# Second layer's gates computed during the second gather and kept in device memory

## The reference, cut to what matters

```python
hd = project_heads(h, w_in[l], rope)          # aq ak av bq bk bv cq ck cv ga gb gc
def merge_branches(hd, ya, yb, yc, wa, wb, wc, wo):
    m = (sigmoid(hd["ga"]) * (ya @ wa) + sigmoid(hd["gb"]) * (yb @ wb)
         + sigmoid(hd["gc"]) * (yc @ wc))
    return m @ wo
x = x + gt1 * merge_branches(...)
h2 = rms_norm(x, g_norm2[l]) * (1.0 + sc2) + sh2
x = x + gt2 * peer_ffn(h2, ...)               # u[e], v[e] of 128 experts for each token
```

## Time and profile before

| | |
|---|---|
| median of 3 runs | 3022.74 us (3022.44 to 3031.11) |
| the profiled execution's own time | 3023.13 us, its span 3021.3 us |
| busy: PE, PE weight loads, DVE, ACT, POOL | 77%, 44%, 61%, 40%, 29% of the span |
| moved by DMA | 1011.33 MB, 335 GB/s in the mean |
| granted TensorE clock, mean | 0.876 of full speed |

### The profile page before, as it was taken

The page is one execution under the profiler, slowest core; times in us unless marked ns, Lnnn a source line. Parts: engine busy times, 40 slices in busy tenths (PEclk is TensorE's granted clock), DMA queues, the critical chain, the costliest instruction groups (busy, mean ns, idle before and its releaser), DMA issues.

```text
span 3021.3 us, 33356 instructions
## 1 busy us (share of the span) xinstructions
PE 2316.5 (77%) x11428; PEld 1343.9 (44%) x11428; DVE 1832.7 (61%) x4465; ACT 1214.4 (40%) x3357; POOL 864.1 (29%) x794
## 2 busy tenths in 40 slices
PE   6999998878779997966555779978998855555555
PEld 4787897434335653521111235426898511111111
DVE  3328655785665556368887645445854777776544
ACT  4215533344653234344344533334643443433333
POOL 0000001333233333334444434320000444444442
PEclk8999998989989998977777899989999987777777
DMA  6631245989999999999999999983153999999996
GB/s 273 222 127 49 90 163 220 416 339 418 421 421 419 420 421 411 413 378 421 406 420 405 419 421 421 421 336 129 46 181 139 396 421 421 421 413 421 417 421 269
DMA packets 139705, 1011.33 MB, mean 335 GB/s; under 512 B 15632, under 2 KB 15760, under 8 KB 17168
## 3 DMA queue, kind: packets, MB, share of 16 engines
q0 software_dynamic: 112032, 810.08, 65.0%
q1 hardware_dynamic: 27216, 196.45, 16.9%
q10 hardware_dynamic: 288, 2.69, 0.2%
HBM read 1008.10 MB, written 1.05 MB: 334 GB/s over the span
## 4 chain that ended last, share of the span: by engine, by line
PE 43%; DMA 30%; DVE 14%; ACT 6%; POOL 3%; issue 3%; ACTq 0%; SPq 0%; POOLq 0%; DVEq 0%
DMA att<-experts_in,att 28%; PE ps L1264 13%; DVE att L2453 5%; PE ps L1123 4%; PE ps L617 4%; PE ps L619 4%; PE ps L618 4%; POOL att L1874 3%; DMA ring<-stream_in 2%; PE ps L906 2%; DVE ring_lo L1927 2%; PE ps L1172 2%; PE ps L872 1%; ACT wt_hi L1370 1%; ACT att L1666 1%
## 5 line engine op out<-in xcount | busy, mean ns | idle before, releaser
L1264 PE MATMUL ps<-att 128*64 128x512 f32 x3072 | 959.3, 758 | 608.9 <-ACT att L1666 608.7
L1874 POOL DMA_INDIRECT att<-experts_in,att x768 | 851.2, 1108 | 1727.2 <-PE ps L1264 1124.1
L2453 DVE CUSTOM_DVE_ANT_0 att<-att 128x1024 f32<-128x1024 f32 x768 | 931.7, 1224 | 623.8 <-DMA att<-experts_in,att 619.4
L1264 PEld LDWEIGHTS ps<-att 128*64 128x64 f32 x3072 | 221.2, 160 | 1233.8 <-ACT att L1666 882.7
L1659 ACT ACTIVATE att<-att 128x1 f32<-128x1 f32 x768 | 154.6, 201 | 992.4 <-DVE att L2453 991.0
L1666 ACT ACTIVATE att<-const,att 128x64 f32<-128x64 f32 x768 | 267.1, 348 | 72.3 <-ACT att L1661 2.2
L1927 DVE TENSOR_TENSOR ring_lo<-ring,wt_hi 128x2048 fp32r<-128x2048 f32 x59 | 135.1, 2292 | 209.4 <-ACT wt_hi L1370 209.4
L1661 ACT ACTIVATE att<-att 128x1 f32<-128x1 f32 x768 | 226.2, 294 | 24.9
L1370 ACT ACTIVATE wt_hi<-ring 128x2048 fp32r<-128x2048 f32 x59 | 112.7, 1909 | 158.1 <-DMA ring<-stream_in 90.4
L617 PE MATMUL ps<-h,wt_hi 128*128 128x256 f32 (+1 forms) x360 | 114.0, 317 | 15.1 <-DVE ring_lo L1927 8.2
L618 PE MATMUL ps<-h,wt_hi 128*128 128x256 f32 (+1 forms) x360 | 111.9, 311 | 0.0
(11 more groups left out here) (267 smaller groups left out, 3609.2 us busy)
## 6 DMA issues: line engine op xcount, KB each, us to landing
ring<-stream_in SPq DMA_DIRECT2D x183, 1024.0 KB, 8.9
att<-experts_in,att POOLq DMA_INDIRECT x768, 12.8
att<-bias_in POOLq DMA_DIRECT2D x16, 256.0 KB, 2.9
spare<-stream_in SPq DMA_DIRECT2D x3, 1024.0 KB, 7.0
x<-x_in ACTq DMA_DIRECT2D x1, 2048.0 KB, 8.1
out<-att SPq DMA_DIRECT2D x1, 1024.0 KB, 3.9
const<-const_in ACTq DMA_DIRECT2D x1, 576.0 KB, 10.3
att<-lambda_in SPq DMA_DIRECT2D x1, 256.0 KB, 9.3
```

The source lines that it names most:

```text
L1264: last = mm(ps[HALF * s:HALF * (s + 1), d, :], diag[:, (m + s) % DIAGS, :], rows[:, (m + s) % SLOTS, D + 512 * d:D + 512 * (d + 1)], start ...
L1874: nc.gpsimd.indirect_dma_start(out=rows[:, m % SLOTS, :], out_offset=None, in_=experts_in, in_offset=bass.IndirectOffsetOnAxis(ap=index[:, ...
L2453: v.tensor_tensor_reduce(out=u_row, in0=u_row, in1=dup[:, n // HK, n % 2, :], scale=1.0, scalar=0.0, op0=ALU.mult, op1=ALU.add, accum_out= ...
```

## The change

The weights of layer 1's merge are laid out by part: 24 gate units (12 pairs), then 24 branch units (6 pairs), the latter sorted by branch and no longer interleaved with gates.

- The gates are computed behind gather 1 from `h1_plain`, in plain float32 matmuls (`lat_gates`), as tanh of half the value on ACT, into one of 4 staging buffers, from which ACT stores each unit (128 KB) to a tensor in device memory, `gate_store`. SP loads all 24 back (3 MB, two DMAs) when gather 1 is over.
- `proj_lat` is cut in two: queries (`lat_queries`), then the gates, then keys and values (`lat_keys`). The chain starts at slot 78 and not at 130; the norm of the first context tile is a norm of its own (number 5), run together with the second half of the gates. All sides are now found by slot 76 (four sides in a block of 24 slots), the picks of the last four quarters are spread over 104 slots. The rotation table is loaded behind row 88, not 124.
- The merge has branch products only: 4 plain matmuls for each item on the unsplit output `yt`, and DVE forms (tanh + 1) x product, with the factor 0.5 put into `yt`. The sigmoid, the split of `h1_plain` and of `yt`, and the splits of 18 pairs go; those of the four pairs of `w_out` remain, the first two in the middle of DVE's products.

```diff
+RUN_UNIT = [0, 0, 0, FIRST_KEY, FIRST_KEY]
+RUN_COUNT = [NU, FIRST_KEY, FIRST_KEY, NU - FIRST_KEY, NU - FIRST_KEY]
+RUN_PAIRS = [QKV_PAIRS, FIRST_KEY // 2, FIRST_KEY // 2, QKV_PAIRS - FIRST_KEY // 2, QKV_PAIRS - FIRST_KEY // 2]
+RUN_TILES = [4, 0, 0, 3, 1]
+FRONT, CTX_Q, LAT_1, LAT_KV, CTX_1 = range(RUNS_OF_UNITS)
+GATES_1 = 3 * DC
+GATE_PAIRS, BRANCH_PAIRS = GATES_1 // 2, GATES_1 // 4
+STAGED = 4
...
-            spread(1, (FIRST_TICKS, 16), (6 * (SIDE_TICKS + PICK_TICKS) + 1, 104)),
+            spread(1, (FIRST_TICKS, 16), (SIDE_TICKS + PICK_TICKS + 1, 18), (SIDE_TICKS + PICK_TICKS, 17), (4 * SIDE_TICKS, 24), (4 * PICK_TICKS, 104)),
...
-             + spread(130, (UPDATE_TICKS, 5), (NORM_TICKS, 13), (proj_ticks(LAT_1), 104)),
+             + spread(78, (NORM_TICKS, 10), (LAT_Q_TICKS, 26), (GATE_TICKS, 26), (GATE_TICKS, 25), (LAT_KV_TICKS, 88)),
...
-    QKV_AT.append(run(QKV_PAIRS, "raw"))
+    dram += QKV_PAIRS
+    QKV_AT.append(run(RUN_PAIRS[LAT_1], "raw", again=first))
+    GATES_AT.append(run(GATE_PAIRS, "raw"))
+    QKV_AT.append(run(RUN_PAIRS[LAT_KV], "raw", again=first + FIRST_KEY // 2))
     QKV_AT.append(run(RUN_PAIRS[CTX_1], "raw", again=first + FIRST_KEY // 2))
-    MERGE_AT.append(run(MERGE_PAIRS, "dense"))
+    MERGE_AT.append(run(BRANCH_PAIRS, "raw"))
...
+        gate_store = nc.dram_tensor("gate_store", (P, GATES_1 * N_LAT), fp32).ap()
...
+        gates_first, gates_last = units(DUP, 16), units(ACTS - 256, 8)
...
+                if p == MERGE_AT[2] + 1:
+                    sp.wait_ge(row_used, PICKS)
+                    for stored in gate_stored:
+                        sp.wait_ge(stored, 16 * (GATES_1 // STAGED))
+                    sp.dma_start(words(DUP, 4096), gate_store[:, 0:4096]).then_inc(gates_back, 16)
+                    sp.dma_start(words(ACTS - 256, 2048), gate_store[:, 4096:6144]).then_inc(gates_back, 16)
...
+            def lat_gates(start, end):
+
+                for g in range(start, end):
+                    if g % 2 == 0:
+                        wait_pair(pe, GATES_AT[0] + g // 2)
+                    if g >= 2:
+                        pe.wait_ge(gate_ready, g - 1)
                     for c in range(DC):
-                        if i == 0:
-                            pe.wait_ge(h_ready, 4 * DC + c + 1)
-                        last = mm(ps[:, 2 + i % 2, 0:N_LAT], raw_slot(p0, i * DC + c), h1_plain[:, c, :],
+                        last = mm(ps[:, 6 + g % 2, 0:N_LAT], raw_slot(GATES_AT[0], g * DC + c), h1_plain[:, c, :],
                                   start=(c == 0), stop=(c == DC - 1))
-                    if i >= FIRST_KEY:
-                        for c in range(DC):
-                            last = mm(ps[:, 2 + i % 2, N_LAT:N_LAT + P], raw_slot(p0, i * DC + c), h1_first[:, c, :],
-                                      start=(c == 0), stop=(c == DC - 1))
-                    last.then_inc(proj_done, 1)
+                    last.then_inc(gate_done, 1)
+                    yield
+                yield from idle(2)
+
+            def first_tile_norm():
+
+                yield from update(1, 0)
+                pe.wait_ge(x_ready, 40)
+                pe.wait_ge(proj_copied, PROJ0[LAT_KV])
+                yield from sums(5)
+                yield from idle(NORM_TICKS - 4)
...
+            def branch_items(start, end):
+
+                p0 = MERGE_AT[2]
+                for g in range(start, end):
+                    if g % 4 == 0:
+                        wait_pair(pe, p0 + g // 4)
+                    if g >= 4:
+                        pe.wait_ge(gated, g - 3)
+                    if g == 2 * DC:
+                        pe.wait_ge(cn_ready, 12)
+                    for c in range(4):
+                        last = mm(ps[:, g % 4, 0:N_LAT], raw_slot(p0, 4 * g + c), yt_l[1][:, 4 * (g // DC) + c, :],
+                                  start=(c == 0), stop=(c == 3))
+                    last.then_inc(branch_done, 1)
...
-                yield from update(1, 0)
-                pe.wait_ge(x_ready, 40)
+                pe.wait_ge(x_ready, 32)
                 yield from sums(4)
                 yield from idle(NORM_TICKS - 4)
-                yield from proj_lat()
+                yield from lat_queries()
+                yield from lat_gates(0, GATES_1 // 2)
+                yield from together(lat_gates(GATES_1 // 2, GATES_1), first_tile_norm())
+                yield from lat_keys()
...
-            head_norm(1)
-            for item in range(1, 6 * DC):
-                merge_item(1, item)
+            pe.wait_ge(y_copied, STEP0[1] + 24)
+            branch_items(0, 4)
+            head_sums(1)
+            branch_items(4, DC)
+            head_spreads(1)
+            branch_items(DC, 3 * DC)
...
-                act.wait_ge(early_moved, 4)
-                split(dense(MERGE_AT[2]))
-                split(dense(MERGE_AT[2]) + 1)
-
-            def lat_high():
-
-                act.wait_ge(dot_done, 2 * PICKS)
-                nc.scalar.activation(h1_lat[0][:, :, :], h1_plain, ACT.Copy).then_inc(lat_hi_ready, 1)
...
+            def lat_gates(start, end):
+                for k in range(start, end + 2):
+                    if k - 2 >= start:
+                        act.wait_ge(gate_ready, k - 1)
+                        act.dma_start(gate_store[:, (k - 2) * N_LAT:(k - 1) * N_LAT], staged[:, (k - 2) % STAGED, :])\
+                            .then_inc(gate_stored[(k - 2) % STAGED], 16)
+                    if start <= k - 1 < end:
+                        act.wait_ge(gate_done, k)
+                        if k - 1 >= STAGED:
+                            act.wait_ge(gate_stored[(k - 1) % STAGED], 16 * ((k - 1) // STAGED))
+                        nc.scalar.activation(staged[:, (k - 1) % STAGED, :], ps[:, 6 + (k - 1) % 2, 0:N_LAT], ACT.Tanh, scale=0.5)\
+                            .then_inc(gate_ready, 1)
+                    yield
...
+            def merge_second():
+                act.wait_ge(early_moved, 4)
+                split(dense(WOUT_AT[2]))
+                split(dense(WOUT_AT[2]) + 1)
+                for j in range(DC):
+                    act.wait_ge(merged, j + 1)
+                    nc.scalar.activation(m1[0][:, j, :], gate_of(2 * DC + j), ACT.Copy).then_inc(m_hi_ready, 1)
...
-                    if r == 1 and n == 124:
+                    if r == 1 and n == 88:
...
-                split(dense(MERGE_AT[2]))
-                split(dense(MERGE_AT[2]) + 1)
-
-            def lat_low():
-
-                dve.wait_ge(lat_hi_ready, 1)
-                v.tensor_tensor(h1_lat[1][:, :, :], h1_plain, h1_lat[0][:, :, :], ALU.subtract).then_inc(lat_lo_ready, 1)
...
+            def products(start, end):
+
+                for g in range(start, end):
+                    dve.wait_ge(branch_done, g + 1)
+                    v.scalar_tensor_tensor(gate_of(g), gate_of(g), 1.0, ps[:, g % 4, 0:N_LAT], ALU.add, ALU.mult)\
+                        .then_inc(gated, 1)
+                    if g >= DC:
+                        dve.wait_ge(gated, g + 1)
+                        last = v.tensor_tensor(gate_of(g), gate_of(g), gate_of(g - DC), ALU.add)
+                        if g >= 2 * DC:
+                            last.then_inc(merged, 1)
+                        else:
+                            link(last)
+
+            def merge_second():
+
+                dve.wait_ge(gates_back, 32)
+                products(0, 4)
+                head_inverses(1)
+                head_diags(1)
+                products(4, DC)
+                heads(1)
+                products(DC, 2 * DC)
+                split(dense(WOUT_AT[2]))
+                split(dense(WOUT_AT[2]) + 1)
                 for j in range(DC):
-                    dve.wait_ge(wout_done, DC * i + j + 1)
-                    for at, s in enumerate(STREAMS[l]):
-                        cols = slice(at * N_LAT, (at + 1) * N_LAT)
-                        last = v.scalar_tensor_tensor(x[:, j, cols], ps[:, j, cols], modcs[l][:, 2 * DC + j, s:s + 1],
-                                                      x[:, j, cols], ALU.mult, ALU.add)
-                    last.then_inc(x_ready, 1)
+                    products(2 * DC + j, 2 * DC + j + 1)
+                    if j:
+                        m_low_second(j - 1)
+                m_low_second(DC - 1)
+                for j in range(WOUT_PAIRS - 2):
+                    split(dense(WOUT_AT[2]) + j + 2)
+                residual(1)
```

More of the change, by code:

```diff
@@ L141, with together @@
 CTX_SIDES = [(0, 2), (0, 3)] + [(1, g) for g in range(4)]
+def together(one, other):
+    for _ in one:
+        next(other)
+        yield
+    ran_out(other)
 def ran_out(work):
@@ L2584, in weight_stream @@
         out.append(wide(part[i]))
-    for j in range(DC):
-        cols = slice(j * P, (j + 1) * P)
-        for gate, branch in ((9, wa), (10, wb), (11, wc)):
-            out += [blocks(part[gate][:, cols]), blocks(branch[:, cols])]
+    columns_of = [slice(j * P, (j + 1) * P) for j in range(DC)]
```

(6 more changed lines are left out.)

381 lines of the change are left out of this document (217 added, 164 removed).

## The result

The changed kernel takes 2984.5 us, the median of 4 runs (2983.9 to 2987.3), against 3022.6 (3020.5 to 3031.1) for the kernel before: a ratio of 0.987, 95% interval 0.9854 to 0.9886. That is 38.1 us less, where 31.4 was forecast. Its profiled execution has a span of 2982.4 us, 38.9 less than that of before.

What follows compares the result with a forecast made beforehand. PE was taken to bound layer 1's merge and DMA bytes the second gather: 3023.1 - 61.7 (merge) - 5.0 (attention's start) + 38.9 (gather) - 4.0 (dips) = 2991.3, so 2991 us; eight in ten 2979 to 3007.

Steps and rivals of the forecast that it cites:

- The trade: Gates move from layer 1's merge, where PE time is paid, to the second gather, where bytes are: 61.7 us for 38.9.
- The signs that the prediction named: Second gather 35 us longer, DMA at 421, mask add 1.2 us after scores, merge 56 us with one 3 us PE gap.
- The merge: Layer 1, last attention copy to output projection: from 117.7 to 56.0 us, a gain of 61.7.
- half clock: Start of layer 1's merge: PE's granted clock falls to half for some 3.5 us, costing 1.7 us.
- The tail: End of the merge: DVE nearly caught up with PE, ACT's rounding behind; 4.9 us, as against 4.7 before.
- The attention's start: Ahead of layer 1's attention: without splits and h's halves on DVE, the first mask add comes earlier, gaining 5.0 us.
- The second gather: Pays 29.9 us for 12 gate weight pairs and 9.0 for 24 stores: 38.9 us lost, before 4.0 given back.
- I give back 4.0: Second gather: thinner later picks on DVE regain 4.0 us of DMA dips, bounds 0 and 10.
- 1: Rival: gate stores cost more than their bytes, 16.1 us for 9.0 or more, no dip regained; 3002 to 3010 us; chance 0.12.
- 2: Rival: 10 us of dips regained instead of 4, or merge stall gone, 4.4 us; 2981 down to 2975; chance 0.12.
- 3: Rival: stores land later than 18 us, ACT waits for staging buffers, row buffers run dry; 3033 at 26 us; chance 0.05.
- 4: Rival: DVE, not PE, would bound the merge, with 30 us of work in 56; 3015 to 3025 us; chance 0.03.

Runs made afterwards that it cites:

- e4: Changed kernel with the unsplit gates made between attention and branch products instead of in the second gather, nothing stored; 3037.7 us.
- a0: The changed kernel run again without edits; 2981.4 us.
- e1: Changed kernel without the 24 gate stores, the two loads that bring them back and the waits for both; 2978.5 us.
- e2: Changed kernel with each gate stored twice, the second time to a second tensor of device memory on the same queue; 2988.6 us.
- e9: Changed kernel with two gates per store, and the second split of w_out's weights moved behind m's last low half; 2980.0 us.
- e6: Changed kernel with the last four quarters' 28 pick ticks in 52 slots instead of 104; 2985.7 us.
- e8: Changed kernel with two gates per store: 12 stores of 256 KB instead of 24 of 128 KB; 2985.3 us.
- e3: Changed kernel with DVE's second split of w_out's weights moved from ahead of product 16 to behind m's last low half; 2980.1 us.
- e7: Changed kernel with two unused 128x2048 subtractions put back on DVE ahead of layer 1's first mask add; 2987.6 us.

## Why the prediction was right, and where it was off

**The trade** held: PE time left a stretch that pays it and came into one that pays bytes. e4 isolates it. The signs that the prediction named came too: DMA at 422 GB/s in the gates' first slots, the first mask add 1.2 us after its scores, one PE gap of 2.8 us before item 20. Priced over all profiles the change brings +37.0 (second gather), -5.9 (start: 50.7 to a mean of 44.8 over those whose start is as in the changed kernel), -0.3 and -67.5 (merge, where the clock holds) or -65.8: 35 to 37 us. The forecast's terms say 31.8. The measured gain is 38.1 and, for a0 beside its own runs of before, 41.2. In the profiled pair the rest is in the head of the program, which the prediction rightly put at nothing: first fetch at 505.9 on average in the three profiles without gates in the gather, at 502.3 in the eleven with them, and by the rows above this is PE's granted clock. Nothing in the change says why it should be granted more there, and equal heads differ by 11 us, so these 4 us are taken for luck; that they are is not shown.

**The merge, 56.0 forecast, 51.9 measured.** By the rows above:
- Matmuls 43.8 + 1.7 of half clock; measured 43.7 with the slow spell, since 7.01 + 6.99 + 20.9 + 8.83. Without it (7.14 in e1 for the last 32 records instead of 8.83) 42.0, or 0.437 us a matmul. The 0.456 was taken from start to start, but in a gather, where a group is eight matmuls and stands between matmuls of another shape:

```profile
663.39 3.72 PE L1008 MATMUL ps<-spare,ring 128*128 128x256 f32 x16
667.04 1.94 PE L1264 MATMUL ps<-att 128*64 128x512 f32 x8
```

  That is 3.65/8. Inside a group two records start 0.216 us apart, here as in the merge, which makes 3.45 us of 16; the other 0.2 us lie at the group's ends, next to the other matmuls. Groups of 16 matmuls take 7.01/16 = 0.438 in the merge above, e4's group of 192 takes 0.433. A long group would have given the right term, some 2 us less.
- The slow spell came, 1.7 us, but behind the stall and not after the attention, and only in some runs. That this term fits the profile is luck.
- Sums and spreads 3.4 for 2.9; stall 2.8 for 2.7.
- **The tail failed**: "DVE ... has nearly caught up by the end, with the rounding on ACT behind: 4.9 us". Measured 1.88. DVE needs some 1.1 us per item (the forecast had 1.4) against PE's 1.73, so it had caught up five products after the split (from item 21 on it waits for PE), and the tail is only product, add, rounding and low half of one item. The 4.7 of before contained a split.

**The attention's start**: 5.0 forecast; the mask add came 6.2 us after the scores before and comes 1.2 after them now, 5.0 as said; scores to last copy went from 91.9 to 86.6, 5.3. The rest of the 5.9 lies ahead of the scores, where PE's granted clock is 0.95 instead of 0.88: 42.7 us between gather and scores instead of 44.5, and e2 and e9, with the change in them, have 0.88 there and 44.4 us.

**The second gather**: 38.9 of bytes less 4.0 of dips forecast, 37.0 measured. Stores 7.1 for 9.0; what is left, 29.9, is what was worked out for the gates' pairs (a difference, so no surer than the 37.0). **The step "I give back 4.0" failed**: thinner picks give nothing back that shows (e4, e6). It also drew on too much: its 13 us of dips come from a window of 765 us whose first 83 belong to the first gather, at 381 GB/s. In the second gather itself, 413 of 421 GB/s over 682 us, 13 us were lost, 7.1 of them at its end, so 6 in dips. It went unnoticed in the total because the stores, taken above their bytes, erred the other way. A dip that is left in the gates' slots is at a quarter's exponentials, where ACT loads tables twice (1746 to 1750 us):

```profile
1746.18 1.28 ACT L1760 ACT_TABLE_LOAD   x1
...
1747.62 0.37 ACT L1604 ACTIVATE att<-ps 128x256 f32<-128x256 f32 x1
1748.00 1.28 ACT L1774 ACT_TABLE_LOAD   x1
```

These loads belong to the exponential and the Gelu behind it; all 24 Tanh (L1604) have none of their own, here or between Gelus. The Trainium skill (ScalarE: Activation LUTs, section Table sets: the hidden batching unit) lists tanh with the exp and sigmoid sets and not with gelu's; the trace of after again disagrees with it.

**The rivals.** 1 is out by e1, e2 and e8. 2 named the right size in the merge, 4.4 us, but for the wrong reason: the stall stayed, and tail and matmuls were shorter; of its dips nothing came back. 3 didn't happen: at the tightest place a store had 15.5 us, not 18, and took at most 9.3. With doubled stores landings of 22 us did hold ACT up, and waits of up to 5.4 us each cost the gather nothing that shows; longer ones weren't tried. 4 is out: DVE works 28.6 us of the 52.

## What to carry to other kernels

Before a move between stages, write down for each what a microsecond of PE and what a megabyte costs there; the form in which the work is done counts less (here it even lost 17 us) than the stage that it stands in. Take the time of a matmul from groups as long as those in which it will stand: short groups between others lose some time at their ends, here 0.456 us against 0.433. Cut the window of a stage at its own end, not at a round number. For a tail ask whether the slower engine is still behind at the last item. When a forecast comes out close, still check it stage by stage: here two errors of 2 to 4 us hid each other, and the head of the program moved by as much with the granted clock.

## What was not expected of the hardware

- Equal programs reached the same instruction, 500 us in, up to 11 us apart from profile to profile, with PE busy 11.0 us longer at a granted clock of 0.94 for 0.96, while the merge repeated within 0.2 us where the clock held. The stretch from gather to scores shows the same: 41.7 us at a granted clock of 1.00 (e3, e7), 44.4 at 0.88 (e2, e9), 46.0 at 0.83 (e4).
- A gap of PE goes before a slow spell in the changed kernel's merge, but is not enough for one. One spell lies behind the stall and one behind the tail; e1 has the same gaps (2.67 and 1.88 us) and neither spell. The one behind the tail (0.57 of full speed from 2246 to 2250 us, matmuls of one shape 0.21 us apart as at 1.2 GHz; the levels are those of the earlier trace rows):

```profile
2246.00:2250.00 4.00, 4.00 (x22) 4.00 (x23) 0.00 (x0) 0.00 (x0) 0.00 (x0) 0.57 0.54 225
```

- Two stores of 128 KB per gate (e2) landed 22 us after their issue at the end of the gates' slots, where a single wide one of 256 KB (e8) was back within 10.0 us. The queue had fallen behind: between 1780 and 1800 us e2 issues eight stores, 1.05 MB, and this is what q10 moved. Why it moved no more, beside the rows and weights, is open.

```profile
q10 hardware_dynamic: 842, 0.77, 11.0%
```
